# Expert gathers one expert further ahead, and a down product in split one-pass parts

## The chip, the cores and the metric

The kernel runs on one core of a Trainium2 chip. The time is the device time of one launch in microseconds. The number of a kernel is the median of several runs. The profile is one execution, recorded by the hardware profiler.

## What is computed

A network of two blocks for one sequence of 512 tokens of width 1024. The first block has two layers; each mixes the tokens by latent attention, an mLSTM and a state-space scan, and ends in a mixture of 16 experts in four groups. The second block has layers with a gated delta rule, a linear recurrence and a feed-forward part. The change touches the experts of the first block alone:

```python
def _hier_moe(x, wg, bg, we, be, w_gate, w_up, w_down):
    glog = (jnp.einsum('bsd,dg->bsg', x, wg) + bg).astype(F32)
    gp, gi = lax.top_k(jax.nn.softmax(glog, -1), 1)
    ...
    ep, ei = lax.top_k(jax.nn.softmax(elog, -1), TOP_K)
    ep = ep / jnp.sum(ep, -1, keepdims=True)
    eid = gi * EXPERTS_PER_GROUP + ei
    combine = jnp.sum(jax.nn.one_hot(eid, N_EXPERTS, dtype=F32) * (gp * ep)[..., None], axis=2)
    h = jax.nn.silu(jnp.einsum('bsd,edf->bsef', x, w_gate)) * jnp.einsum('bsd,edf->bsef', x, w_up)
    h = h * combine[..., None].astype(h.dtype)
    return jnp.einsum('bsef,efd->bsd', h, w_down)
```

Each token goes to two of the 16 experts. An expert has gate and up weights of 1024 x 256 each and down weights of 256 x 1024, all fp32.

## The kernel before

All engines run the stage `experts` as five queues of their own, written out by hand and joined by semaphores; nothing reorders them. The stage runs once per layer (its outer loop makes one pass when no expert has more than 128 tokens, as here), over experts e = 0 to 15.

For one expert, in the order of the data:

- **GpSimd** gathers up to 128 rows of the tokens into XE by an indirect DMA (`gather`, L1174); XE has two buffers, so gather e waits until expert e-2 has been transposed (`row_t`). The row numbers are in `table`.
- **SyncE** loads the gate/up weights (GU, 2 MB, four buffers, two of them in the tile `raw`, one in XT) and the down weights (DN, 1 MB, four buffers).
- **TensorE** transposes XE into a bank (`rows_t`, L1204). ScalarE copies it as a rounded high part XS (L1278) and VectorE writes the rest as the low part (L1321). The weights are split likewise: ScalarE's `high` (L1271) and VectorE's `low` (L1315) fill WS, each half of an expert in one 128x2048 instruction.
- **TensorE** multiplies in 24 one-pass matmuls (`gate_up_of`, L1216): high x high, high x low and low x high, listed in `TERMS`. ScalarE applies silu (L1295), VectorE multiplies gate and up into H (L1357), TensorE transposes H (`hidden_t`, L1226), ScalarE copies it to HT (L1307).
- **TensorE** forms the down product (`down_of`, L1237) in plain fp32, 4 matmuls which the trace shows as 8. ScalarE copies the lower half to YE and VectorE the upper one (`out_home`, L1284 and L1328).
- **GpSimd** scatters YE to the table `mixed_dram` (`scatter`, L1181).

The index of the rows comes from TensorE (`table_of`, L1245), from one-hot rows that VectorE writes (`hot_rows`, L1334), and VectorE turns it into integers (`index`, L1338).

What sets the order: in round e, TensorE does gate/up of e, the table of e+3, down of e-1, the transposes of rows e+2 and then of H e. GpSimd does gather e+3, then scatter e. ScalarE does the first half of `high` of e+1, silu e, the second half, YE of e-1, the XS of e+2, HT of e.

Of the kernel before, what the change touches and what calls it, by code (L numbers as in the profile page):

```python
# [1136 lines left out]
def experts(nc, m, r, layer):  # L1137
# [7 lines left out]
    names = ("hot_row", "table_done", "indexed", "dve_step", "xe_in0", "xe_in1", "ye_out0", "ye_out1", "gu_in0", "gu_in1", "gu_in2", "gu_in3", "dn_in0", "dn_in1", "dn_in2", "dn_in3", "row_t", "xe_high", "xe_low",  # L1145
             "w_high", "w_low", "gate_up", "silu_done", "hidden", "ht_done", "ht_home", "down", "ye_act", "ye_dve")
    with stage(nc, "experts", *names) as (block, sems):
        hot_row, table_done, indexed, dve_step, xe_in0, xe_in1, ye_out0, ye_out1, gu_in0, gu_in1, gu_in2, gu_in3, dn_in0, dn_in1, dn_in2, dn_in3, row_t, xe_high, xe_low, \
            w_high, w_low, gate_up, silu_done, hidden, ht_done, ht_home, down, ye_act, ye_dve = sems
        xe_in, ye_out = (xe_in0, xe_in1), (ye_out0, ye_out1)  # L1150
        gu_in, dn_in = (gu_in0, gu_in1, gu_in2, gu_in3), (dn_in0, dn_in1, dn_in2, dn_in3)
        GU = KD * S

        @block.sync
        def _(sp):

            for e in range(NE):
                b = e % 4

                if e >= 4:  # L1160
                    sp.wait_ge(w_low, 2 * (e - 3))
                sp.dma_start(r.GU[b], m.d["w_exp"][bass.ds(layer, 1), e, :, 0:GU].rearrange("a p n -> p (a n)")).then_inc(gu_in[b], 16)
                if e >= 4:
                    sp.wait_ge(down, 2 * (e - 3))
                sp.dma_start(r.DN[:, b, :], m.d["w_exp"][bass.ds(layer, 1), e, :, GU:].rearrange("a p n -> p (a n)")).then_inc(dn_in[b], 16)

        @block.gpsimd
        def _(pool):
# [9 lines left out]
            def scatter(e):  # L1178
                pool.wait_ge(ye_act, e + 1)
                pool.wait_ge(ye_dve, e + 1)  # L1180
# [15 lines left out]
        def _(pe):  # L1196
# [24 lines left out]
            def hidden_t(e):  # L1221
                pe.wait_ge(hidden, e + 1)
                if e:
                    pe.wait_ge(ht_home, e)
# [1414 lines left out]
```

## Time and profile before

| | us |
|---|---|
| median of 3 runs | 2199.01 (2198.95 to 2201.67) |
| the profiled execution | 2196.01 |
| its span, first to last instruction | 2194.2 |
| TensorE busy in the span | 1761.4 (80%) |
| VectorE, ScalarE, GpSimd busy | 1099.9, 804.6, 675.9 |
| mean granted TensorE clock | 0.896 |

The busy shares are means over stages with different limits, so they say little about one stage. The two expert stages together take under a fifth of the span; what counts is which wait in them ends last. A line number is that of the kernel before. "Idle before" is an engine's idle time ahead of an instruction, with what ended it.

### The profile page before, as it was taken

The page shows a single profiled execution, that of the slowest core. Times are in us where ns is not written, and L with a number is a line of the kernel's source. Part 1 is how long each engine was busy: PE and PEld are TensorE (multiplying, and loading weights), DVE is VectorE, ACT ScalarE, POOL GpSimd, SP SyncE. Part 2 cuts the span into 40 slices and gives each one's busy share as a digit, 9 for nine tenths or more (in the row PEclk, how much of TensorE's full clock was granted, in tenths as well). Part 3 has the DMA queues.
Part 4 walks back from the last instruction along what each step waited for, and adds up shares of the span by engine and source line. Part 5 has one row for each costly group of instructions (what it writes and reads, how often), then busy time and mean ns, then how long its engine had stood idle before and what let it go on. Part 6 is the DMA issues. An engine that isn't in the chain of part 4 may idle for free. (4 is left out here: it accounts for less than half of the span.)

```text
span 2194.2 us, 22094 instructions
## 1 busy us (share of the span) xinstructions
PE 1761.4 (80%) x7850; PEld 1318.8 (60%) x7850; DVE 1099.9 (50%) x1623; ACT 804.6 (37%) x1196; POOL 675.9 (31%) x351
## 2 busy tenths in 40 slices
PE   4999885759991899986858893499697487999997
PEld 3876533646660786731646661488377376888885
DVE  2836565455656555654646665391455413242241
ACT  2246554134542235665215452322635322111111
POOL 2426524011110444632301110243342113444442
PEclk9999996869995999997959996799789798999998
DMA  4201111077744311020148862320000204222221
GB/s 168 77 31 39 44 34 58 39 292 304 307 165 156 121 48 41 1 77 20 39 178 346 318 255 112 116 96 23 18 1 1 72 6 154 96 96 96 96 76 48
DMA packets 40473, 233.80 MB, mean 107 GB/s; under 512 B 9316, under 2 KB 9700, under 8 KB 20660
## 3 DMA queue, kind: packets, MB, share of 16 engines
q1 hardware_dynamic: 31012, 215.42, 26.1%
q0 software_dynamic: 9216, 16.80, 2.0%
q8 instruction: 59, 0.97, 0.2%
q10 hardware_dynamic: 144, 0.26, 0.1%
q14 instruction: 42, 0.34, 0.1%
HBM read 226.00 MB, written 23.23 MB: 114 GB/s over the span
## 5 line engine op out<-in xcount | busy, mean ns | idle before, releaser
L2134 POOL TENSOR_TENSOR WS<-ring,WS 128x2048 fp32r<-128x2048 f32 x32 | 154.6, 4833 | 228.5 <-ACT WS L2126 228.5
L252 PE MATMUL bank<-XS,WS 128*128 128x512 f32 x864 | 201.8, 396 | 19.9 <-POOL WS L448 19.9
L252 PEld LDWEIGHTS bank<-XS,WS 128*128 128x128 f32 x864 | 165.3, 192 | 56.0 <-POOL WS L448 21.2
L1216 PE MATMUL bank<-WS,XS 128*128 128x512 f32 x768 | 190.3, 405 | 2.2 <-DVE XS L1321 2.2
L2155 PE MATMUL bank<-XS,WS 128*128 128x512 f32 x768 | 177.1, 393 | 14.3 <-POOL WS L2134 14.3
L2173 PE MATMUL bank<-WS,US 128*128 128x512 f32 x768 | 174.7, 389 | 0.0
L2155 PEld LDWEIGHTS bank<-XS,WS 128*128 128x128 f32 x768 | 145.7, 190 | 44.9 <-issue 14.5
L1216 PEld LDWEIGHTS bank<-WS,XS 128*128 128x128 f32 x768 | 147.3, 195 | 33.3 <-DVE XS L1321 3.0
L2126 ACT CAST WS<-ring 128x2048 fp32r<-128x2048 f32 x32 | 61.2, 1913 | 283.2 <-PE bank L2155 150.0
L2173 PEld LDWEIGHTS bank<-WS,US 128*128 128x128 f32 x768 | 144.2, 188 | 29.9
L1519 PE MATMUL bank<-XS,WS 128*128 128x512 f32 (+1 forms) x600 | 138.6, 394 | 13.9 <-POOL WS L1573 13.9
L1519 PEld LDWEIGHTS bank<-XS,WS 128*128 128x128 f32 (+1 forms) x600 | 112.3, 187 | 39.8 <-POOL WS L1573 14.1
L448 POOL TENSOR_TENSOR WS<-raw,WS 128x2048 fp32r<-128x2048 f32 x20 | 92.9, 4646 | 110.9 <-ACT WS L306 110.8
L1181 POOL DMA_INDIRECT mixed_rows<-YE,table x32 | 32.2, 1005 | 288.1 <-DVE YE L1328 147.0
L1237 PE MATMUL bank<-DN,HT 128*128 128x512 f32 x256 | 117.2, 600 | 1.0 <-issue 1.0
L662 POOL TENSOR_SCALAR XT<-XT,RC 128x512 f32<-128x512 f32 x64 | 100.2, 1567 | 46.9 <-DVE RC L627 46.7
L961 PE MATMUL bank<-WS,XS 128*128 128x512 f32 x384 | 92.8, 406 | 26.4 <-POOL WS L1022 26.4
L1315 DVE TENSOR_TENSOR WS<-raw,WS 128x2048 fp32r<-128x2048 f32 x32 | 73.2, 2291 | 60.5 <-ACT WS L1271 60.5
L961 PEld LDWEIGHTS bank<-WS,XS 128*128 128x128 f32 x384 | 75.7, 198 | 45.8 <-issue 29.5
L2204 DVE TENSOR_TENSOR X<-X,bank 128x512 f32<-128x512 f32 x32 | 22.0, 688 | 144.4 <-PE bank L2173 144.4
L1573 POOL TENSOR_TENSOR WS<-ring,WS 128x2048 fp32r<-128x2048 f32 (+1 forms) x13 | 58.8, 4524 | 76.1 <-ACT WS L1530 76.1
L183 PE MATMUL bank<-ident,X 128*128 128x128 f32 x128 | 23.2, 367 | 70.6 <-issue 48.0
(472 smaller groups left out, 3346.3 us busy)
## 6 DMA issues: line engine op xcount, KB each, us to landing
raw<-in_w_exp SPq DMA_DIRECT2D x16, 2048.0 KB, 10.6
DN<-in_w_exp SPq DMA_DIRECT2D x32, 1024.0 KB
ring<-in_w_ff SPq DMA_DIRECT2D x32, 1024.0 KB, 4.8
raw<-in_w_in SPq DMA_DIRECT2D x20, 1024.0 KB, 4.9
GU<-in_w_exp SPq DMA_DIRECT2D x8, 2048.0 KB, 10.5
XT<-in_w_exp SPq DMA_DIRECT2D x8, 2048.0 KB, 10.4
ring<-in_w_in SPq DMA_DIRECT2D x12, 1024.0 KB, 4.8
raw<-in_w_out SPq DMA_DIRECT2D x8, 1024.0 KB, 5.0
```

The costliest lines, as they stand in the source:

```text
L252: last = pe.matmul(m.ps[g % 8][:, :], WS[:, i % 2, hw, at:at + P], XS[:, hx, k, :], start=(step == 0), stop=(step == 3 * KD - 1))
L448: pool.tensor_tensor(WS[:, i % 2, 1, :], m.raw[:, i % 4, :], WS[:, i % 2, 0, :].bitcast(F32), ALU.subtract).then_inc(w_low, 1)
L662: pool.tensor_scalar(PR[:, i % 4, :], PR[:, i % 4, :], a.RC[:, i % 4:i % 4 + 1], None, ALU.mult).then_inc(probs_normed, 1)
L961: last = pe.matmul(m.ps[2 * t + half][:, :], XS[:, hx, 4 * kh + k, t * P:(t + 1) * P], WS[:, 2 * kh + half, hw, k * S:(k + 1) * S], start= ...
L1216: last = pe.matmul(m.ps[2 + e % 2][:, :], r.XS[:, e % 2, hx, 4 * half + k, :], r.WS[:, half, hw, k * S:(k + 1) * S], start=(half == 0 and ...
L1237: last = pe.matmul(m.ps[5 + half][:, :], r.HT[:, e % 2, f * P:(f + 1) * P], r.DN[:, e % 4, at:at + S], start=(f == 0), stop=(f == 1))
L1315: dve.tensor_tensor(r.WS[:, half, 1, :], r.GU[e % 4][:, half * 4 * S:(half + 1) * 4 * S], r.WS[:, half, 0, :].bitcast(F32), ALU.subtract). ...
L1519: last = pe.matmul(m.ps[u % 8][0:n, :], q.WS[:, i % 2, hw, at:at + n], b.XS[:, hx, k, :], start=(step == 0), stop=(step == 3 * KD - 1))
L2126: act.copy(f.WS[:, q % 2, 0, :], f.ring[:, q % 4, :]).then_inc(w_high, 1)
L2134: pool.tensor_tensor(f.WS[:, q % 2, 1, :], f.ring[:, q % 4, :], f.WS[:, q % 2, 0, :].bitcast(F32), ALU.subtract).then_inc(w_low, 1)
L2155: last = pe.matmul(m.ps[mine + u % 4][:, :], f.WS[:, q % 2, hw, k * 256 + c * P:k * 256 + (c + 1) * P], f.XS[:, hx, k, :], start=(n == 0), ...
L2173: last = pe.matmul(bank[:, :], f.US[:, hx, 4 * kh + k, t * P:(t + 1) * P], f.WS[:, q % 2, hw, k * S:(k + 1) * S], start=(kh == 0 and n == ...
```

## The change

Three things change in the stage `experts`.

1. The gathers: GpSimd issues gather e+4 in round e (and gather 3 in round 0), ahead of scatter e. The table, the one-hot rows and the index of e+4 move to round e on TensorE and VectorE with it.
2. The down product: HT and the down weights are split into a high and a low part. HT's high part is ScalarE's copy, its low part a subtraction on VectorE. DN's high part is written by ScalarE (`part_high`, two 128x1024 casts), its low part by GpSimd (`part_low`, two 128x1024 subtractions, between gather e+4 and scatter e). The parts lie in the new tile DS, which has one buffer, and TensorE does 12 one-pass matmuls. HT has one buffer for each part.
3. The rest: both halves of YE are copied by ScalarE. DN has two buffers instead of four; SyncE loads DN e after the low part of e-2 is written, and GU e+2 behind it.

In the rows below, numbers at the start are lines of the kernel they belong to.

GpSimd at the start of the stage, before (XE is the gather, mixed_rows the scatter):

```order
L1167 UNCONDITIONAL_BRANCH
L1174 DMA XE<-x_rows,table 128x1024 x4
L1181 DMA mixed_rows<-YE,table 1024x1024
L1174 DMA XE<-x_rows,table 128x1024
L1181 DMA mixed_rows<-YE,table 1024x1024
```

and after:

```order
L1171 UNCONDITIONAL_BRANCH
L1178 DMA XE<-x_rows,table 128x1024 x5
L1192 TENSOR_TENSOR DS<-DN,DS 128x1024 x2
L1185 DMA mixed_rows<-YE,table 1024x1024
L1178 DMA XE<-x_rows,table 128x1024
L1192 TENSOR_TENSOR DS<-DN,DS 128x1024 x2
```

Five gathers now stand ahead of the first scatter, and two subtractions stand between each gather and the next scatter.

ScalarE over one expert in the middle of the stage, before (WS: gate/up weights, high part; GB: silu; XS: rows, high part):

```order
L1271 CAST WS<-raw 128x2048
L1295 ACTIVATE GB<-bank 128x256
L1271 CAST WS<-raw 128x2048
L1284 COPY YE<-bank 128x512
L1278 CAST XS<-bank 128x512 x2
L1307 COPY HT<-bank 128x256
```

and after:

```order
L1290 CAST WS<-raw 128x2048
L1322 ACTIVATE GB<-bank 128x256
L1290 CAST WS<-raw 128x2048
L1304 COPY YE<-bank 128x512 x2
L1297 CAST XS<-bank 128x512 x2
L1334 CAST HT<-bank 128x256
L1311 CAST DS<-DN 128x1024 x2
```

The two casts of the down weights stand behind HT, ahead of the next expert's weights.

The diff, cut to its core:

```diff
@@ sync
-            for e in range(NE):
-                b = e % 4
-
+            def gate_up_in(e):
                 if e >= 4:
                     sp.wait_ge(w_low, 2 * (e - 3))
...
+            gate_up_in(0)
+            gate_up_in(1)
+            for e in range(NE):
+                if e >= 2:
+                    sp.wait_ge(down_low, 2 * (e - 1))
+                sp.dma_start(r.DN[:, e % 2, :], m.d["w_exp"][bass.ds(layer, 1), e, :, GU:].rearrange("a p n -> p (a n)")).then_inc(dn_in[e % 2], 16)
+                if e + 2 < NE:
+                    gate_up_in(e + 2)
@@ gpsimd
+            def part_low(e):
+                for f in range(2):
+                    pool.wait_ge(down_high, 2 * e + f + 1)
+                    cols = slice(f * D, (f + 1) * D)
+                    pool.tensor_tensor(r.DS[:, 1, cols], r.DN[:, e % 2, cols], r.DS[:, 0, cols].bitcast(F32), ALU.subtract).then_inc(down_low, 1)
...
             for e in range(NE):
-                if e + 3 < NE:
-                    gather(e + 3)
+                if e == 0:
+                    gather(3)
+                if e + 4 < NE:
+                    gather(e + 4)
+                part_low(e)
                 scatter(e)
@@ tensor
             def down_of(e):
-                pe.wait_ge(dn_in[e % 4], 16 * (e // 4 + 1))
-                pe.wait_ge(ht_home, e + 1)
+                pe.wait_ge(ht_low, e + 1)
                 for half in range(2):
                     if e:
-                        pe.wait_ge((ye_act, ye_dve)[half], e)
+                        pe.wait_ge((ye_low, ye_up)[half], e)
+                    n = 0
                     for f in range(2):
+                        if half == 0:
+                            pe.wait_ge(down_low, 2 * e + f + 1)
                         at = f * D + half * S
-                        last = pe.matmul(m.ps[5 + half][:, :], r.HT[:, e % 2, f * P:(f + 1) * P], r.DN[:, e % 4, at:at + S], start=(f == 0), stop=(f == 1))
+                        for hw, hx in TERMS:
+                            last = pe.matmul(m.ps[5 + half][:, :], r.HT[:, hx, f * P:(f + 1) * P], r.DS[:, hw, at:at + S], start=(n == 0), stop=(n == 5))
+                            n += 1
                     last.then_inc(down, 1)
@@ scalar
             def out_home(e):
...
+                for half in range(2):
+                    act.wait_ge(down, 2 * e + half + 1)
+                    if e >= 2:
+                        act.wait_ge(ye_out[e % 2], 16 * (e // 2))
+                    act.copy(r.YE[:, e % 2, half * S:(half + 1) * S], m.ps[5 + half][:, :]).then_inc((ye_low, ye_up)[half], 1)
+
+            def part_high(e):
+                act.wait_ge(dn_in[e % 2], 16 * (e // 2 + 1))
+                if e:
+                    act.wait_ge(down, 2 * e)
+                for f in range(2):
+                    act.copy(r.DS[:, 0, f * D:(f + 1) * D], r.DN[:, e % 2, f * D:(f + 1) * D]).then_inc(down_high, 1)
...
                 act.wait_ge(ht_done, e + 1)
-                if e >= 2:
-                    act.wait_ge(down, 2 * (e - 1))
-                act.copy(r.HT[:, e % 2, :], m.ps[4][:, 0:2 * P]).then_inc(ht_home, 1)
+                if e:
+                    act.wait_ge(down, 2 * e)
+                act.copy(r.HT[:, 0, :], m.ps[4][:, 0:2 * P]).then_inc(ht_high, 1)
+                part_high(e)
@@ vector
-            def out_home(e):
-                dve.wait_ge(down, 2 * e + 2)
...
+                dve.wait_ge(ht_high, e + 1)
+                if e:
+                    dve.wait_ge(down, 2 * e)
+                dve.tensor_tensor(r.HT[:, 1, :], m.ps[4][:, 0:2 * P], r.HT[:, 0, :].bitcast(F32), ALU.subtract).then_inc(ht_low, 1)
```

## Rows read from the trace of the kernel before

**Rows 1.** Waits in the expert stages, layer one, then two: total, times, longest.

```profile
PE bank L1204 <- DMA XE<-x_rows,table: 15.3, 11, 3.6
...
PE bank L1204 <- DMA XE<-x_rows,table: 17.2, 12, 3.2
```

**Rows 2.** Timeline of one period: start, length, engine, line, operation, idle before.

```profile
566.94 5.72 PE L1216 MATMUL bank<-WS,XS 128*128 128x512 f32 x24
...
568.24 1.01 POOL L1174 DMA_INDIRECT XE<-x_rows,table  x1 [0.31 <-issue]
...
570.03 1.91 ACT L1271 CAST WS<-raw 128x2048 fp32r<-128x2048 f32 x1 [2.11 <-PE bank L1216]
...
572.86 3.68 PE L1237 MATMUL bank<-DN,HT 128*128 128x512 f32 x8
...
574.90 2.29 DVE L1315 TENSOR_TENSOR WS<-raw,WS 128x2048 fp32r<-128x2048 f32 x1 [0.30 <-ACT WS L1271]
...
577.18 0.68 DVE L1328 COPY YE<-bank 128x512 f32<-128x512 f32 x1
...
577.37 1.09 PE L1204 MATMUL bank<-ident,XE 128*128 128x128 f32 x8 [0.83 <-DMA XE<-x_rows,table]
...
578.06 1.07 ACT L1278 CAST XS<-bank 128x512 fp32r<-128x512 f32 x2 [2.62 <-PE bank L1204]
...
578.43 5.72 PE L1216 MATMUL bank<-WS,XS 128*128 128x512 f32 x24
...
578.72 1.01 POOL L1181 DMA_INDIRECT mixed_rows<-YE,table  x1 [9.46 <-PE bank L1204]
579.02 0.39 ACT L1307 COPY HT<-bank 128x256 f32<-128x256 f32 x1
...
580.03 1.02 POOL L1174 DMA_INDIRECT XE<-x_rows,table  x1 [0.31 <-issue]
```

**Rows 3.** Timeline of TensorE near the end of layer one's stage.

```profile
630.49 3.59 PE L1237 MATMUL bank<-DN,HT 128*128 128x512 f32 x8
633.92 1.04 PE L1204 MATMUL bank<-ident,XE 128*128 128x128 f32 x8
```

**Rows 4.** Timeline: first gate/up matmul, gather of expert 3, last scatter, layer one.

```profile
467.89 0.80 PE L1216 MATMUL bank<-WS,XS 128*128 128x512 f32 x1 [1.01 <-DVE XS L1321]
...
483.05 0.99 POOL L1174 DMA_INDIRECT XE<-x_rows,table  x1 [14.34 <-DVE table L1338]
...
659.17 0.97 POOL L1181 DMA_INDIRECT mixed_rows<-YE,table  x1 [3.42 <-DVE YE L1328]
```

**Rows 5.** Durations elsewhere: first ns min/median/max, then busy us, mean ns.

```profile
L448 POOL TENSOR_TENSOR WS<-raw,WS x20: 4499/4618/4847, 35.4 to 813.9; 128x2048 fp32r<-128x2048 f32 x20
...
L653 POOL TENSOR_TENSOR QS<-QT,QS 128x512 fp32r<-128x512 f32 x14 | 17.9, 1282 | 0.0
...
L1450 ACT ACTIVATE XN<-X 128x1024 f32<-128x1024 f32 x8 | 8.3, 1043 | 27.6 <-PEq L76 21.7 <-PEq L2403 5.9
```

**Rows 6.** Output projection: GpSimd and VectorE side by side; VectorE's min/median/max.

```profile
361.37 4.52 POOL L1022 TENSOR_TENSOR WS<-raw,WS 128x2048 fp32r<-128x2048 f32 x1 [14.38 <-ACT WS L1007]
...
361.84 4.60 DVE L973 TENSOR_TENSOR XS<-XT,XS 128x512 fp32r<-128x512 f32 x1 [1.39 <-ACT XS L1002]
...
L973 DVE TENSOR_TENSOR XS<-XT,XS x16: 683/2646/5104, 358.0 to 1055.7; 128x512 fp32r<-128x512 f32 x16
```

**Rows 7.** TensorE after two pauses; in between a window: length, busy, PEclk, DMA, GB/s.

```profile
518.09 1.67 PE L1204 MATMUL bank<-ident,XE 128*128 128x128 f32 x8 [1.98 <-DMA XE<-x_rows,table]
...
519.84 6.66 PE L1216 MATMUL bank<-WS,XS 128*128 128x512 f32 x24
...
520.00:522.00 2.00, 2.00 (x6) 1.58 (x6) 1.72 (x6) 0.66 (x2) 0.62 (x1) 0.54 1.08 459
...
1185.97 1.09 PE L1204 MATMUL bank<-ident,XE 128*128 128x128 f32 x8 [3.23 <-DMA XE<-x_rows,table]
```

**Rows 8.** Window at the start of layer one's stage; last columns PEclk, DMA share, GB/s.

```profile
470.00:500.00 30.00, 25.07 (x106) 19.17 (x106) 15.88 (x23) 14.56 (x17) 3.03 (x3) 0.88 0.98 403
```

More of the change, by code:

```diff
@@ L1137, in experts @@
 def experts(nc, m, r, layer):
[L1145 to L1146 removed]
+    names = ("hot_row", "table_done", "indexed", "dve_step", "xe_in0", "xe_in1", "ye_out0", "ye_out1", "gu_in0", "gu_in1", "gu_in2", "gu_in3", "dn_in0", "dn_in1", "row_t", "xe_high", "xe_low",
+             "w_high", "w_low", "gate_up", "silu_done", "hidden", "ht_done", "ht_high", "ht_low", "down_high", "down_low", "down", "ye_low", "ye_up")
     with stage(nc, "experts", *names) as (block, sems):
[L1148 to L1149 removed]
+        hot_row, table_done, indexed, dve_step, xe_in0, xe_in1, ye_out0, ye_out1, gu_in0, gu_in1, gu_in2, gu_in3, dn_in0, dn_in1, row_t, xe_high, xe_low, \
+            w_high, w_low, gate_up, silu_done, hidden, ht_done, ht_high, ht_low, down_high, down_low, down, ye_low, ye_up = sems
         xe_in, ye_out = (xe_in0, xe_in1), (ye_out0, ye_out1)
[L1151 removed]
+        gu_in, dn_in = (gu_in0, gu_in1, gu_in2, gu_in3), (dn_in0, dn_in1)
         GU = KD * S
@@ L1155, in _ @@
         def _(sp):
-            for e in range(NE):
-                b = e % 4
+            def gate_up_in(e):
                 if e >= 4:
                     sp.wait_ge(w_low, 2 * (e - 3))
[L1162 to L1165, printed above, removed]
+                sp.dma_start(r.GU[e % 4], m.d["w_exp"][bass.ds(layer, 1), e, :, 0:GU].rearrange("a p n -> p (a n)")).then_inc(gu_in[e % 4], 16)
+            gate_up_in(0)
[6 more added lines that the diff above has]
+                    gate_up_in(e + 2)
         @block.gpsimd
@@ L1223, in hidden_t @@
                 if e:
-                    pe.wait_ge(ht_home, e)
+                    pe.wait_ge(ht_low, e)
                 for f in range(2):
@@ L1254, in _ @@
                     rows_t(1)
-                if e + 3 < NE:
-                    table_of(e + 3)
+                if e == 0:
+                    table_of(3)
+                if e + 4 < NE:
+                    table_of(e + 4)
                 if e:
@@ L1280, in out_home @@
             def out_home(e):
-                act.wait_ge(down, 2 * e + 1)
-                if e >= 2:
-                    act.wait_ge(ye_out[e % 2], 16 * (e // 2))
-                act.copy(r.YE[:, e % 2, 0:S], m.ps[5][:, :]).then_inc(ye_act, 1)
+                for half in range(2):
[9 more added lines that the diff above has]
+                    act.copy(r.DS[:, 0, f * D:(f + 1) * D], r.DN[:, e % 2, f * D:(f + 1) * D]).then_inc(down_high, 1)
             high(0, 0)
@@ L1349, in _ @@
             for e in range(NE):
-                if e + 3 < NE:
-                    hot_rows(e + 3)
+                if e == 0:
+                    hot_rows(3)
+                if e + 4 < NE:
+                    hot_rows(e + 4)
                 if e + 1 < NE:
@@ L1361, in _ @@
                     low(e + 1, 1)
-                if e + 3 < NE:
-                    index(e + 3)
-                if e:
-                    out_home(e - 1)
+                if e == 0:
+                    index(3)
+                if e + 4 < NE:
+                    index(e + 4)
                 if e + 2 < NE:
                     rows_low(e + 2)
-            out_home(NE - 1)
+                dve.wait_ge(ht_high, e + 1)
+                if e:
+                    dve.wait_ge(down, 2 * e)
+                dve.tensor_tensor(r.HT[:, 1, :], m.ps[4][:, 0:2 * P], r.HT[:, 0, :].bitcast(F32), ALU.subtract).then_inc(ht_low, 1)
             dve.wait_ge(hot_row, NE * NT)
```

13 lines of the change are left out of this document (5 added, 8 removed).

## The prediction

> **What bounds the kernel now.** I read the views in this order: the waits of the expert stages, the timeline of one expert in steady state, then durations, first and last instructions, and the granted clock. The only thing TensorE waits for repeatedly there is the gathered rows XE: 15.3 us in layer one, 17.2 in layer two [rows 1]. The timeline shows why [rows 2]. One expert runs from the gate/up matmuls at 566.94 to those at 578.43, 11.49 us: 5.92 to the first down matmul, then the down product, then a wait of 0.83 until XE lands, then 1.06 from the transposes (577.37) to the next gate/up. Those transposes use a gather issued at 568.24, 9.1 us earlier. That gather stands behind the scatter of an earlier expert, which waits for VectorE's copy of YE (577.18 in this period), which waits its turn behind VectorE's low part of the weights (574.90). So two loops are nearly equal: TensorE's own work and the gather behind the scatter. Where XE was in time, the down product is 3.43 long from start to start [rows 3], so TensorE alone would take 5.92 + 3.43 + 1.06 = 10.4. GpSimd does 2.3 us of work per expert and is otherwise idle. The stage of layer one runs from 467.89 to the start of its last scatter, 659.17: 191.3 us [rows 4]; layer two is taken alike.
>
> **What the change removes.** Gather e+4 is queued ahead of scatter e. Its own condition (the transposes of e+2 are done) is met about one period earlier than now, so XE has a period of slack beside its 9.1 us and the waits of [rows 1] go. The down product becomes 12 one-pass matmuls. At 5.72/24 = 0.238 each [rows 2] they take 2.86 in place of 3.43, a gain of 0.57. VectorE loses a 0.68 copy. If nothing else came, TensorE's period would be 5.92 + 2.86 + 1.06 = 9.84.
>
> **What it adds.** ScalarE gets a second YE copy (half of the 1.07 for two XS parts [rows 2], 0.55) and two 128x1024 casts; the only 128x1024 row without bias is 1.04 [rows 5], taken as 1.0. VectorE gets a 128x256 subtraction from a bank, hidden while it waits. GpSimd gets two 128x1024 subtractions. Their price lies between half of the fastest 128x2048 one, 2.25, and the line through 1.28 for 512 and 4.62 for 2048, 2.39, a little more if disturbed [rows 5]; I take 2.35. On SyncE, DN(e) waits for the subtractions of e-2, and the gate/up weights of e+2 are queued behind it, so they are requested about 20 us ahead of use where now it is over three periods. Both transfers with a gather and a scatter are some 3.7 MB, 9.2 us at the 403 GB/s of [rows 8]. I count nothing for them: about 8 us are left, and a period longer than now relieves the queue.
>
> **The new loop.** GpSimd works in order: scatter, gather, low part f0, low part f1. Time 0 is the end of f1 of one expert.
> - TensorE, released by f1, has 9 of 12 down matmuls left: 0.15 + 9 x 0.238 = 2.3. (0.15 is my estimate for one release: the XS copy starts 0.69 after the transposes, of which half take 0.54 [rows 2].)
> - ScalarE copies the second half of YE: 0.15 + 0.55, at 3.0. The scatter starts 0.86 after YE (577.86 to 578.72 [rows 2]): 3.86. The gather starts 1.31 later and takes 1.02: 6.2. Then f0 starts at 6.35. The gap of 0.15 is an estimate between 0.05 and the 0.31 between two transfers.
> - f0 ends at 8.7. Without interference f1 ends at 11.05.
>
> ScalarE's casts don't limit f0. The HT copy is over 2.04 after the transposes start [rows 2], at 4.34, the casts at 5.35 and 6.35.
>
> **Interference.** VectorE's low part of WS (L1315) reads two SBUF operands and takes 2.29 [rows 2]. In the output projection VectorE runs such an instruction, XS<-XT,XS, beside GpSimd's WS<-raw,WS. Alone it takes 0.68. Started 0.47 after GpSimd's it takes 4.60, and ends 0.55 after GpSimd's end, with a maximum of 5.10 [rows 6]. So they exclude one another, instruction by instruction, and take turns. The Trainium skill, "SBUF — State Buffer", section "SBUF: two separate sides", says that such a pair is an exclusive lock held for the whole instruction and names VectorE operations with two SBUF inputs. By its wording VectorE's reads of a bank stay free, which no row I use shows; if they too had to wait, the sum would be some 1 us per expert higher.
>
> Where does the request fall? The transposes start at 2.3, gate/up at 3.36. ScalarE's first cast of the next weights starts 3.09 after that (566.94 to 570.03 [rows 2]), at 6.45, and ends at 8.36. VectorE asks at 8.4, while f0 holds the lock until 8.7. VectorE goes next, until 11.0; f1 then runs to **13.35**. The second VectorE part is ready at about 11.4 and waits for f1, harmlessly, since gate/up of the next expert starts 3.36 after f1. Period 13.35 against 11.49 now, and TensorE pauses about 3.5 us inside each down product (three matmuls done at 10.0, resumed at 13.5).
>
> **Sum of a stage**, from the first gate/up matmul:
> - First f1: gather 3 starts at 15.2 [rows 4], gather 4 is over at 17.5, and f0 and f1 need 4.7 with one or two VectorE parts between: 24.6 to 26.5 or a little less; 25.
> - 11 periods of 13.35: 146.9.
> - Two periods without a gather: f0 follows the first cast at 5.5 and f1 ends at 10.2, before VectorE gets its turn; 10.3 each, 20.6. Two more, also without transposes: 9.75 each, 19.5.
> - From the last f1 to the last scatter: 0.15 + 2.14 + 0.15 + 0.55 + 0.86 = 3.85.
>
> Together 215.8, against 191.3: +24.5 per layer, **+49**. The profiled execution took 2196.0 (span 2194.2), the median is 3.0 higher: 2199.0 + 49 = **2248**.
>
> **Rivals.**
> - **VectorE just misses f0** (ask after 8.7; the margin is 0.3). Then f1 ends at 11.05, but VectorE's parts and the index behind them slip, the next gather starts 0.9 late, and in the next period VectorE is in time: 14.2. Mean 12.6. That saves 0.75 x 11 x 2 = 16: 2232; with the lower prices of both bounds (2.25 and 0.05) about 2216. For it: the small margin. Against: slips on GpSimd help VectorE be in time.
> - **No price for the lock** (the other side). If the two engines don't collide here, the period is 11.05, the first f1 at 22.3: 22.3 + 121.6 + 20.6 + 19.5 + 3.85 = 187.9, so 3.4 less per layer: 2192. GpSimd's loop has then replaced the gather's, almost at the same length, and the longer tail (f0 and f1 behind the last scatters) eats most of the gain. It decides if VectorE's request falls after f1 has begun in every period. Against it: [rows 6].
> - **TensorE becomes the bound**, if GpSimd's subtractions overlapped its transfers or weren't waited for: 9.84, so 1.65 less over 13 periods and some 3 us per layer for the longer waits of the first experts (up to 3.6 [rows 1]): 2199 - 49 = 2150. Against it: one queue in order.
> - **The clock falls in the pauses.** After a pause of 1.98 the granted clock was 0.54, the 1.2 GHz level: the transposes took 1.67 in place of 1.09, the 24 matmuls 6.66 in place of 5.72, together 1.5. After one of 3.23 it didn't fall and they took 1.09 [rows 7]. The new pause is 3.5, in 13 periods per layer. Half of them: +20, 2268; all of them: +39, 2287. A dearer subtraction (2.5) or a gap of 0.31 adds 3 to 4 us per layer.
> - **The gather isn't further ahead in effect:** XE has two buffers as before. It still starts a period earlier, and even at 15 us to landing it would be in time, so this costs nothing.
>
> **Chances.** The lock with VectorE in time 0.50 (2248, by the prices' bounds 2235 to 2262); just missing 0.17 (2216 to 2232); falls of the clock or dearer GpSimd work on top 0.21 (2262 to 2290); no price for the lock 0.09 (2192); TensorE the bound 0.03 (2150). The range leaves out the last two and the end of the clock's case: 2212 to 2284. A measurement of this kernel tells about 0.2%, 4.4 us, from no change. Faster: 0.03 and over half of 0.09, 0.08; same: the rest of it, and a little of the second case, 0.05; slower 0.87.
>
> **What would show it.** In the profile after: the wait for XE gone; TensorE waiting for GpSimd's DS inside the down product in nearly every expert; GpSimd's second 128x1024 subtraction recorded at about 4.6 and the first at 2.35; VectorE's low part of WS sometimes 2.29, sometimes longer; periods of about 13.35, then four shorter; granted clock at 1.00 for most of the stage. I would be wrong if the subtractions were both at 2.3 (no lock), if periods alternated between 11 and 14, or if TensorE waited for something else: weights that land late, or ScalarE.

## The result and the profile after

| | before | after |
|---|---|---|
| median, same chip | 2199.52 us (2198.95 to 2201.67) | 2255.85 us (2250.22 to 2257.06) |
| the profiled execution / its span | 2196.01 / 2194.2 | 2250.22 / 2248.5 |
| mean granted clock | 0.896 | 0.876 |
| experts, layer one, first gate/up to last scatter | 191.3 | 216.8 |
| experts, layer two | 190.1 | 216.7 |

The ratio is 1.0249, interval 1.0230 to 1.0268: slower, by 56 us. Of the 54.3 us that the span grew, 25.5 and 26.6 are the two stages. The other 2.2 lie outside them: 0.8 more ahead of the first stage, 2.0 more ahead of the second, 0.6 less behind it. In layer one gather 0 lands 10.7 us after its issue instead of 9.2; a second load of gate/up weights now stands ahead of DN 0.

Three groups of the page of the changed kernel, GpSimd's subtraction, the down product and VectorE's one-hot rows (busy us, mean ns | idle before and who ended it):

```profile
L1192 POOL TENSOR_TENSOR DS<-DN,DS 128x1024 fp32r<-128x1024 f32 x64 | 151.2, 2387 | 1.0
...
L1253 PE MATMUL bank<-DS,HT 128*128 128x512 f32 x384 | 133.0, 507 | 18.6 <-POOL DS L1192 18.6
...
L1356 DVE TENSOR_SCALAR HOT<-IOTA,POS 128x128 fp32r<-128x128 f32 x128 | 138.5, 1150 | 3.1 <-PEq L76 3.1
```

The subtraction costs what was expected. The third row wasn't expected: a one-hot row, a 128x128 tile, takes 1150 ns in the mean, where most take 280. TensorE's waits over the whole run of the changed kernel (total, times, longest) point at the same rows:

```profile
PE bank L1262 <- DVE HOT L1356: 50.1, 22, 5.6
...
PE bank L1217 <- DMA XE<-x_rows,table: 18.8, 2, 9.5
PE bank L1253 <- POOL DS L1192: 18.6, 12, 4.8
PE bank L1262 <- DVE table L1360: 11.3, 6, 5.0
```

The wait for XE of [rows 1] has gone: two are left, each stage's very first. In its place TensorE waits 22 times for a one-hot row. It waits for DS only 12 times, though the prediction had it wait in nearly every expert.

One period of the changed kernel, from its timeline (start, length, engine, line, operation, idle before); it answers to [rows 2]:

```profile
566.12 6.01 DVE L1356 TENSOR_SCALAR HOT<-IOTA,POS 128x128 fp32r<-128x128 f32 x4
566.25 1.05 POOL L1178 DMA_INDIRECT XE<-x_rows,table  x1 [0.31 <-issue]
567.32 4.73 POOL L1192 TENSOR_TENSOR DS<-DN,DS 128x1024 fp32r<-128x1024 f32 x2
...
569.83 0.39 PE L1262 MATMUL bank<-VAL,HOT 128*128 128x2 f32 x3
...
572.06 2.28 DVE L1343 TENSOR_TENSOR WS<-raw,WS 128x2048 fp32r<-128x2048 f32 x1
572.19 0.27 PE L1262 MATMUL bank<-VAL,HOT 128*128 128x2 f32 x1 [1.97 <-DVE HOT L1356]
...
572.33 4.58 PE L1253 MATMUL bank<-DS,HT 128*128 128x512 f32 x12
...
576.94 0.59 ACT L1304 COPY YE<-bank 128x512 f32<-128x512 f32 x1 [1.45 <-PE bank L1253]
...
578.39 1.01 POOL L1185 DMA_INDIRECT mixed_rows<-YE,table  x1 [6.35 <-PE bank L1217]
...
579.71 1.05 POOL L1178 DMA_INDIRECT XE<-x_rows,table  x1 [0.31 <-issue]
580.79 4.72 POOL L1192 TENSOR_TENSOR DS<-DN,DS 128x1024 fp32r<-128x1024 f32 x2
...
585.51 2.28 DVE L1343 TENSOR_TENSOR WS<-raw,WS 128x2048 fp32r<-128x2048 f32 x1
```

Narrow windows of the same timeline split two of these rows, the last one-hot row and the first subtraction:

```profile
580.17 5.42 DVE L1356 TENSOR_SCALAR HOT<-IOTA,POS 128x128 fp32r<-128x128 f32 x1
```

```profile
580.79 2.40 POOL L1192 TENSOR_TENSOR DS<-DN,DS 128x1024 fp32r<-128x1024 f32 x1
```

The two subtractions are called f0 and f1 as in the prediction, the DMA of GpSimd ahead of them is the gather. Read from the end of f1 at 572.05 (567.32 + 4.73): 0.28 until the down product starts, 4.61 until ScalarE's copy of YE (576.94), 0.59 for the copy, 0.86 to the scatter, 1.32 to the gather, 1.08 to f0, 4.72 for f0 and f1. Together **13.46**, and seven of the stage's intervals between gate/up starts are of this length. The two subtractions run back to back, undisturbed. What is held up is VectorE: it asked for its fourth one-hot row 0.46 us after the gather began, and the row ended only when gather, f0 and f1 were over. TensorE's table product (L1262) needs that row, and it stands in TensorE's queue ahead of the down product, so none of the 12 matmuls runs before f1's end. The first three rows had got through.

The clock, in windows (length, busy PE, PEld, DVE, ACT, POOL with counts, granted clock, DMA share, GB/s):

```profile
572.00:573.00 1.00, 0.81 (x4) 0.66 (x5) 1.00 (x2) 0.20 (x1) 0.04 (x1) 0.87 0.00 0
573.00:574.00 1.00, 1.00 (x4) 0.81 (x3) 1.00 (x1) 0.00 (x0) 0.00 (x0) 0.50 0.89 164
...
576.00:577.00 1.00, 1.00 (x7) 0.82 (x6) 0.94 (x2) 0.06 (x1) 0.00 (x0) 0.92 1.10 467
```

After the pause of 1.97 the granted clock falls to 0.50, the 1.2 GHz level, for about the length of the down product: 12 matmuls take 4.58. At 519.70, in a shorter round of the same stage and at a granted clock of 1.00, they take 3.00. In the nine longest rounds of layer one (13.4 or more) they take 4.5 to 5.5, together 15 us more than at 3.00 each, out of the 25.5 that the stage grew. The clock is back at full before gate/up.

At the stage's start, two rows in the first round, one of VectorE and one of TensorE, from the timeline:

```profile
480.53 2.29 DVE L1343 TENSOR_TENSOR WS<-raw,WS 128x2048 fp32r<-128x2048 f32 x1 [0.64 <-ACT WS L1290]
...
482.94 1.01 PE L1262 MATMUL bank<-VAL,HOT 128*128 128x2 f32 x4 [4.95 <-DVE table L1360]
```

Round 0 now makes two tables. The second must wait until VectorE has read the first, and that `index` stands in VectorE's queue behind a low part of the weights. TensorE stands for 4.95 us.

### The profile page after: what moved, and what is told of

Its sections match the earlier page's. It is cut to its first block and busy times, and to the rows that moved or that the text cites. A ratio compares the mean times of both kernels' runs of the same rounds, so it can differ in the third digit from the quotient of the medians.

```text
span 2248.5 us, 22572 instructions
## 1 busy us (share of the span) xinstructions
PE 1777.6 (79%) x7978; PEld 1369.4 (61%) x7978; DVE 1210.7 (54%) x1623; ACT 882.6 (39%) x1292; POOL 831.5 (37%) x415
## 5 line engine op out<-in xcount | busy, mean ns | idle before, releaser
L1192 POOL TENSOR_TENSOR DS<-DN,DS 128x1024 fp32r<-128x1024 f32 x64 | 151.2, 2387 | 1.0
L1253 PE MATMUL bank<-DS,HT 128*128 128x512 f32 x384 | 133.0, 507 | 18.6 <-POOL DS L1192 18.6
L1356 DVE TENSOR_SCALAR HOT<-IOTA,POS 128x128 fp32r<-128x128 f32 x128 | 138.5, 1150 | 3.1 <-PEq L76 3.1
L1253 PEld LDWEIGHTS bank<-DS,HT 128*128 128x128 f32 x384 | 93.1, 251 | 45.5 <-POOL DS L1192 13.9
```

The lines of the kernel that those rows point to most:

```text
L1192: pool.tensor_tensor(r.DS[:, 1, cols], r.DN[:, e % 2, cols], r.DS[:, 0, cols].bitcast(F32), ALU.subtract).then_inc(down_low, 1)
L1253: last = pe.matmul(m.ps[5 + half][:, :], r.HT[:, hx, f * P:(f + 1) * P], r.DS[:, hw, at:at + S], start=(n == 0), stop=(n == 5))
L1356: dve.tensor_scalar(r.HOT[:, e % 2, t, :], m.IOTA[:, :], r.POS[:, t, e:e + 1], None, ALU.is_equal).then_inc(hot_row, 1)
```

## The experiments

Two theories stood at the outset. **Turns**, the prediction's: VectorE and GpSimd exclude one another and take turns, so VectorE's low part of the weights gets in between f0 and f1. **No turn**, formed from the profile: VectorE gets no turn between GpSimd's back-to-back instructions; the one-hot row is blocked from the gather to f1's end, and because the table stands ahead of the down product, the whole product and a fall of the clock go onto GpSimd's loop.

| kernel | median us | ratio to before (95%) | stages, layer one / two |
|---|---|---|---|
| gathers alone | 2180.40 | 0.9887 to 0.9931 | 177.0 / 177.1 |
| split alone | 2259.36 | 1.0263 to 1.0297 | 217.0 / 215.4 |
| one-hot rows moved | 2222.05 | 1.0087 to 1.0121 | 202.5 / 201.1 |
| table behind down product | 2229.38 | 1.0111 to 1.0172 | 205.2 / 206.1 |
| subtractions in quarters | 2338.74 | 1.0587 to 1.0655 | 246.5 / 248.4 |
| gather between f0 and f1, rows moved | 2243.35 | 1.0160 to 1.0233 | 212.5 / 211.0 |
| fills instead of subtractions | 2223.67 | 1.0070 to 1.0140 | 201.3 / 201.2 |
| the same, rows moved | 2225.35 | 1.0066 to 1.0147 | 197.2 / 202.3 |
| low parts on VectorE | 2170.46 | 0.9862 to 0.9896 | 170.2 / 170.1 |
| low parts on VectorE, index earlier | 2162.89 | 0.9799 to 0.9841 | 167.5 / 167.4 |
| gathers alone, index earlier | 2165.26 | 0.9814 to 0.9860 | 173.5 / 173.6 |
| low parts on VectorE, index earlier, loads reordered | 2160.20 | 0.9788 to 0.9832 | 168.3 / 168.1 |

The ratios are to the kernel before as it was measured again beside each kernel (medians 2198.85 to 2201.88); the stages are those of the profiled executions. A stage's length is the sharper measure: the granted clock in the code ahead of it, which the change leaves as it is, differs between the profiles, and the first stage starts anywhere from 467 to 476 (474 to 476 where the clock from 300 to 350 us was 0.76, 467 to 471 where it was 0.79 to 0.84), the second 488 to 497 after the end of the first. Rounds are counted from one start of gate/up to the next.

### The two parts, each alone

The kernel before with the gathers, tables, one-hot rows and indices of the change:

```diff
@@ gpsimd (tensor and vector alike)
-                if e + 3 < NE:
-                    gather(e + 3)
+                if e == 0:
+                    gather(3)
+                if e + 4 < NE:
+                    gather(e + 4)
                 scatter(e)
```

> The kernel before with the gathers (and the table, one-hot rows and index with them) one expert further ahead, nothing else. If the waits for XE are what the profile of before shows, they vanish and TensorE's own 10.4 us per expert remain: about 15 us less per layer, although the first round gets 5 us longer, since the table of expert 4 now waits for the index of expert 3 (4.95 us in the changed kernel). That gives about 2170. Rival: the transfers (3.7 MB per expert at 403 GB/s, 9.2 us) or the weights come late at that pace, and the gain shrinks to under 10 us in all, 2190 or more.

Measured 2180.40, 0.9% faster. Between the first and the last rounds its intervals are 10.4, ten times in a row, the length that the prediction gave TensorE alone. Of the waits of [rows 1] one is left in layer one:

```profile
PE bank L1206 <- DMA XE<-x_rows,table: 7.3, 1, 7.3
```

It is the stage's very first. The first round takes 17.2 here too, as the second table waits for the first index; the expectation had counted that. The two stages are 27.3 shorter, near the 30 expected. But the profiled execution is only 15.5 shorter: the first stage starts 5.9 later than before, and 7.5 more lie between the two, in code that is the same. Whether that comes with the change or is the spread between executions isn't known.

The changed kernel with the gathers back at e+3, on all three engines:

```diff
-                if e == 0:
-                    gather(3)
-                if e + 4 < NE:
-                    gather(e + 4)
+                if e + 3 < NE:
+                    gather(e + 3)
                 part_low(e)
```

> The changed kernel with the gathers back at three experts ahead: the split down product alone. If GpSimd's loop (scatter, gather, two subtractions, VectorE's one-hot rows behind them, the down product) sets the period, 13.4 us stay, XE lands in time at that pace anyway, and only the first round gets shorter by the 4.95 us that TensorE waited for the index of expert 3: about 2246. Rival: the shorter distance brings waits for XE back, 1 us or more per expert, 2270 or more.

Measured 2259.36, period 13.45, stages of 217.0 and 215.4. The whole loss is the split's. The gathers, worth 13 to 14 us a stage alone, bring nothing beside it: GpSimd's loop contains its gather wherever the gather's number stands. The first round is shorter (12.5), as expected, but one more long round makes up for it, so the 2246 expected didn't come.

### Who is blocked, and who waits behind it

The one-hot rows moved out of GpSimd's busy stretch, to just behind `index`:

```diff
                 if e == 0:
                     hot_rows(3)
-                if e + 4 < NE:
-                    hot_rows(e + 4)
+                    hot_rows(4)
...
                     index(e + 4)
+                if e + 5 < NE:
+                    hot_rows(e + 5)
```

> The changed kernel with VectorE's one-hot rows written one round earlier, in the idle 1.1 us ahead of its XS low parts, when GpSimd computes nothing. Theory of the shared port as predicted: TensorE no longer waits for the one-hot rows, but VectorE's low part of the weights, now asked for during GpSimd's first subtraction, gets its turn between the two, so the second subtraction is recorded at about 4.6 us and the period stays near 13.35 (or 12.6 where it alternates): 2235 to 2255. Rival: only the one-hot rows are blocked, and the low parts of the weights run beside GpSimd at 2.28; then the period is GpSimd's own 11.1 to 11.3 and the time about 2203.

Measured 2222.05, between what the theory (2235 to 2255) and its rival (2203) gave: 34 us of the loss are gone, but the rounds alternate between 13.2 and 10.8, mean 12.0. The timeline of one round:

```profile
570.97 4.72 POOL L1192 TENSOR_TENSOR DS<-DN,DS 128x1024 fp32r<-128x1024 f32 x2
...
572.33 5.51 DVE L1343 TENSOR_TENSOR WS<-raw,WS 128x2048 fp32r<-128x2048 f32 x1 [1.22 <-ACT WS L1290]
...
573.50 0.94 PE L1253 MATMUL bank<-DS,HT 128*128 128x512 f32 x3 [0.15 <-POOL DS L1192]
...
575.74 2.54 PE L1253 MATMUL bank<-DS,HT 128*128 128x512 f32 x6 [1.30 <-POOL DS L1192]
```

This is the prediction's own situation: VectorE asks for a low part of WS at 572.33, while f0 runs. It got no turn between f0 and f1. It lasted 5.51, until 2.15 behind f1's end, and f0 and f1 together took their 4.72. That refutes "turns" for this pair. "No turn" has the blocking right but didn't foresee the rest: the nine matmuls behind f1 (the view ends at 578) took 3.82 at a lower clock (0.56 in the window 576 to 578), and in the 10.8 rounds 2.34 after a shorter pause. Such falls make up 1.5 of the 2.4 between the two kinds of round. The one-hot rows' blocking is real: moving them alone was worth 1.5%.

The rows stay, and TensorE's table moves behind the down product:

```diff
-                if e + 4 < NE:
-                    table_of(e + 4)
                 if e:
                     down_of(e - 1)
+                if e + 4 < NE:
+                    table_of(e + 4)
```

> The changed kernel, GpSimd's subtractions and VectorE's order as they are, with TensorE's table matmuls of expert e+4 queued behind the down product of e-1 instead of ahead of it. The one-hot rows stay blocked (5.4 us), but no down product stands behind them. If that queue order is how the port costs time, the down product starts at once, its pause falls from 2.0 before all 12 matmuls to one before the last nine, the clock falls less often, and the period goes from 13.46 to 11.2 to 12.0: 2195 to 2222. Rival: VectorE's weights, held back by the same blocking, come late for the next gate/up; then it stays above 2240.

Measured 2229.38, 26 us less than the changed kernel and a little outside what was expected. VectorE's rows are blocked as long as ever, but three matmuls now run before f1's end, so that nine are left:

```profile
572.14 5.83 DVE L1356 TENSOR_SCALAR HOT<-IOTA,POS 128x128 fp32r<-128x128 f32 x4
...
577.73 2.34 PE L1253 MATMUL bank<-DS,HT 128*128 128x512 f32 x9 [0.98 <-POOL DS L1192]
```

In other rounds of this kernel the nine matmuls take 3.91, at the lower clock, and its intervals spread from 10.4 to 14.0. So what stands behind the blocked row in TensorE's queue carries about half of the loss, with GpSimd's 4.7 us as they were.

### What kind of exclusion

Each subtraction cut into four, to offer VectorE more boundaries:

```diff
-                    pool.tensor_tensor(r.DS[:, 1, cols], r.DN[:, e % 2, cols], r.DS[:, 0, cols].bitcast(F32), ALU.subtract).then_inc(down_low, 1)
+                    for c in range(4):
+                        cols = slice(f * D + c * 256, f * D + (c + 1) * 256)
+                        last = pool.tensor_tensor(r.DS[:, 1, cols], r.DN[:, e % 2, cols], r.DS[:, 0, cols].bitcast(F32), ALU.subtract)
+                    last.then_inc(down_low, 1)
```

> The changed kernel with each of GpSimd's two 128x1024 subtractions cut into four of 128x256 (0.6 us each), back to back. In the changed kernel and with the one-hot rows moved, VectorE waited through both subtractions though there was a boundary between them. Theory A: GpSimd keeps the pair as long as its instructions follow back to back; then nothing changes but the fixed cost of six more instructions, VectorE's fourth one-hot row still takes about 5.4 us, and the time is 2256 or slightly more. Theory B: VectorE gets its turn at any boundary and missed the only one by accident of timing; with seven boundaries its longest one-hot row falls under 2 us, TensorE no longer waits for the table, and the time falls to 2235 or less.

The letters there aren't this section's order: its theory A is "no turn", its B is "turns".

Measured 2338.74, 6% slower than before; rounds alternate between 11.9 and 18.75. Its timeline, one round of each kind:

```profile
567.71 6.40 DVE L1358 TENSOR_SCALAR HOT<-IOTA,POS 128x128 fp32r<-128x128 f32 x4
...
568.25 5.57 POOL L1193 TENSOR_TENSOR DS<-DN,DS 128x256 fp32r<-128x256 f32 x8
...
581.11 9.71 POOL L1193 TENSOR_TENSOR DS<-DN,DS 128x256 fp32r<-128x256 f32 x8
...
583.15 2.31 DVE L1345 TENSOR_TENSOR WS<-raw,WS 128x2048 fp32r<-128x2048 f32 x1 [0.45 <-ACT WS L1292]
```

In the first kind a one-hot row, asked for at 568.10 while the gather runs, waits through all eight pieces (5.82). In the second, one-hot rows are served between pieces (0.77 each), VectorE's low part of WS too, and GpSimd's eight take 9.71 instead of 5.57. Neither theory holds as stated: a boundary between two GpSimd instructions passes the turn in some cases and not in others. What decides it wasn't found.

With the one-hot rows moved as above, the gather placed between f0 and f1:

```diff
+                part_low(e, 0)
                 if e + 4 < NE:
                     gather(e + 4)
-                part_low(e)
+                part_low(e, 1)
                 scatter(e)
```

> The kernel with the one-hot rows moved (2222), and the gather of e+4 placed between GpSimd's two subtractions instead of ahead of them. If the pair is free while GpSimd writes the descriptors of a gather (1 us), VectorE's low part of the weights starts in that gap and then holds the second subtraction off for its 2.28 us: the second subtraction is recorded at 3 us or more, VectorE's at 2.3 to 3.5 in place of 4.7 to 5.5. By the sum of the loop (f1 later by about 2.3) the time would be 2235 to 2250. Rival: the gather holds VectorE off as well, nothing is lost to a turn, and the time stays near 2222.

Measured 2243.35, in the range expected; rounds of 14.2 and 11.2. Two rounds of its timeline differ by half a microsecond in when VectorE asks:

```profile
566.35 1.02 POOL L1178 DMA_INDIRECT XE<-x_rows,table  x1
...
566.93 4.99 DVE L1343 TENSOR_TENSOR WS<-raw,WS 128x2048 fp32r<-128x2048 f32 x1 [3.39 <-ACT WS L1290]
...
577.96 1.02 POOL L1178 DMA_INDIRECT XE<-x_rows,table  x1 [0.16 <-issue]
578.06 2.29 DVE L1343 TENSOR_TENSOR WS<-raw,WS 128x2048 fp32r<-128x2048 f32 x1 [1.22 <-ACT WS L1290]
579.01 3.54 POOL L1191 TENSOR_TENSOR DS<-DN,DS 128x1024 fp32r<-128x1024 f32 x1
```

Asked 0.10 after the gather's start, VectorE is served at once and f1 is held up (3.54 instead of 2.37). Asked 0.58 after it, VectorE waits through the rest of the gather and all of f1. So a turn can be had shortly after a gather's start, and not later. By itself a gather costs little: in the kernel before, with no subtraction behind it, no one-hot row took more than 0.50, asked 0.54 after the gather's start and done at its end.

```profile
L1334 DVE TENSOR_SCALAR HOT<-IOTA,POS x128: 266/279/503, 453.0 to 1293.4; 128x128 fp32r<-128x128 f32 x128
```

GpSimd's subtractions replaced, from expert 1 on, by three fills of a spare tile (about 0.97, 0.97 and 0.43 us), which read nothing and leave the low part of the down weights out:

```diff
+                    else:
+                        scratch(slice(0, D))
+                        scratch(slice(0, D))
+                        scratch(slice(0, 400))
+                        pool.wait_ge(pool_step, scratched[0])
+                        pool.sem_inc(down_low, 1)
```

> The changed kernel, but from expert 1 on GpSimd fills a spare 128x1024 tile (some 2.3 us of fills in place of each subtraction) and reads nothing; the low part of the down weights is left at that of expert 0, so that part of the computation is left out. GpSimd is as long busy, so its loop stays. If it is reading SBUF that blocks VectorE, the one-hot rows are free, TensorE doesn't wait for the table, the clock stays up, and the period is GpSimd's own 11.1 to 11.3: 2200 to 2210. If writing blocks the one-hot rows as well (they run at two elements a cycle), it stays at 2245 to 2260.

And the same with the one-hot rows moved:

> The same fills in place of the subtractions (the same part of the computation left out), with the one-hot rows moved out of GpSimd's way. What may still collide is VectorE's low part of the weights, with two SBUF inputs. If such an instruction is held off only by a GpSimd instruction that reads SBUF, it takes 2.28 us every time and the time is 2195 to 2208, GpSimd's loop alone; if also by one that writes, it takes 4.5 to 5.5 as with the subtractions and the time is near 2222.

Measured 2223.67 and 2225.35. The first lies between its two ranges; the second is where its rival had it (near 2222), but not for the rival's reason. The groups of the first (ns least, median, most; first and last start) and one row of its timeline show what the fills block:

```profile
L1371 DVE TENSOR_SCALAR HOT<-IOTA,POS x128: 276/282/2445, 452.3 to 1299.4; 128x128 fp32r<-128x128 f32 x128
...
L1358 DVE TENSOR_TENSOR WS<-raw,WS x32: 2283/2293/2293, 462.0 to 1316.4; 128x2048 fp32r<-128x2048 f32 x32
```

```profile
568.89 1.83 DVE L1371 TENSOR_SCALAR HOT<-IOTA,POS 128x128 fp32r<-128x128 f32 x1
```

Instructions that only write still block a one-hot row (one tensor operand in SBUF): the one shown waits for the rest of the gather and one fill, 1.84 at most over the run, and is done 0.09 after that fill. (The 2445 ns are beside expert 0's subtraction, which stays.) Between two fills GpSimd waits for a semaphore and is idle for 0.06, between two subtractions it isn't. Fills never block the low part of WS (two operands in SBUF), though it ran beside them in almost every round: 2293 at most in 32. Against subtractions the same instruction took up to 5.56. So for the two-operand form it is GpSimd's reading that excludes. With rows moved and fills, the period is 11.38, GpSimd's own loop, and layer one's stage 197.2, 5.7 above a loop without exclusion (187.9 by the prediction, plus 11 x 0.33 for the longer period). Part of the rest is the clock: in one round of 13.0 nine matmuls take 3.91 at 0.56, in the others 2.34, after the same pause of 1.35. Layer two has four such rounds and a stage of 202.3, so the median is no better than with the rows in place.

### The low parts elsewhere, and the first round

VectorE writes the low parts of the down weights, behind HT's low part:

```diff
@@ gpsimd
-                part_low(e)
                 scatter(e)
@@ vector
                 dve.tensor_tensor(r.HT[:, 1, :], m.ps[4][:, 0:2 * P], r.HT[:, 0, :].bitcast(F32), ALU.subtract).then_inc(ht_low, 1)
+                part_low(e)
```

> The changed kernel with the low parts of the down weights written by VectorE (2 x 1.15 us) in place of GpSimd, ahead of its one-hot rows. GpSimd computes nothing, so nothing can block VectorE. If GpSimd's subtractions are the cause, directly or through the port, the loss goes and the gain of the shorter down product shows: periods of 10.0 to 10.5, 2160 to 2175. Rival: the loss is in the split itself (ScalarE's added 2.6 us, the single buffer DS, the later requests of the weights): then it stays above 2220.

Measured 2170.46, 1.2% faster than before, as expected. The rest of the split is as in the changed kernel, so ScalarE's added work, the single buffer DS and the later loads aren't what cost the time. One period (9.76: gate/up at 561.10 and 570.86) of its timeline:

```profile
563.10 2.36 DVE L1349 TENSOR_TENSOR DS<-DN,DS 128x1024 fp32r<-128x1024 f32 x2
...
565.38 0.87 DVE L1355 TENSOR_SCALAR HOT<-IOTA,POS 128x128 fp32r<-128x128 f32 x4
...
567.03 2.98 PE L1246 MATMUL bank<-DS,HT 128*128 128x512 f32 x12
```

VectorE does both subtractions in 2.36, half of GpSimd's 4.72, the four one-hot rows take 0.87, and the 12 matmuls 2.98 at full clock. TensorE is the bound again, at 9.76 where the prediction's rival had 9.84.

The index of expert 3 ahead of VectorE's second low part of the first round, in that kernel and in the one with the gathers alone:

```diff
-                if e + 1 < NE:
-                    low(e + 1, 1)
                 if e == 0:
                     index(3)
+                if e + 1 < NE:
+                    low(e + 1, 1)
```

> The kernel with the low parts on VectorE (2170), and in round 0 the index of expert 3 taken ahead of VectorE's second low part of the weights instead of behind it. TensorE's table of expert 4 waits for that index, 4.9 us in the first round. If that wait is real time, 2 to 3 us less per layer: 2164 to 2167. Rival: the gather of expert 2 lands at about the same moment and the first rounds stay as long: 2170.

> The kernel with the gathers alone further ahead (2180), with the same earlier index of expert 3: 2174 to 2178, or 2180 if the first rounds are bound by the gather.

Measured 2162.89 and 2165.26, the first a little under its range, the second clearly. The first interval is 13.8 in both instead of 16.6 and 17.2, and the stages are 2.8 and 3.5 shorter. Of the 15 us that the second median fell, the stages account for 7; its first stage starts 6.7 earlier than with the gathers alone. Between these two kernels the split with VectorE's low parts is worth 6.0 and 6.2 us a stage; the medians differ by 2.4 with overlapping intervals, so in the whole time it isn't shown.

Last, the kernel with the low parts on VectorE and the index earlier, with SyncE's first three loads in the order of the kernel before: GU 0, DN 0, GU 1, then GU 2, DN 1, GU 3.

```diff
             gate_up_in(0)
-            gate_up_in(1)
             for e in range(NE):
+                if e == 1:
+                    gate_up_in(2)
...
-                if e + 2 < NE:
+                if e == 0:
+                    gate_up_in(1)
+                elif e + 2 < NE and e >= 2:
                     gate_up_in(e + 2)
+                elif e == 1:
+                    gate_up_in(3)
```

> The low parts on VectorE, the early index, and the down weights of expert 0 loaded ahead of the gate/up weights of expert 1, as in the kernel before, so that the first gather meets less traffic (it took 1.2 to 1.5 us longer to land in the changed kernel). 1 us less per layer than with the early index alone: 2162 to 2165, under both kernels and about 1.6% under the kernel before. Rival: the gate/up weights of expert 1 are then late for ScalarE and the time is that of the early index alone or above.

Measured 2160.20, ratio 0.9810 (0.9788 to 0.9832), the lowest median of all and 1.9% under the kernel before. Against the one without the reordering the intervals overlap, so its gain isn't shown: from the issue of gather 0 to gate/up it takes 11.8 and 12.6 instead of 13.3 and 13.7, but the stages are 0.9 and 0.8 longer.

## Why the prediction was nearly right, and where it wasn't

It said 2248 (2212 to 2284); it was 2255.85. Of the 8 us between, 3 are the stages (+25.5 and +26.6 where it had +24.5 for each), 2 what lies outside them, and 3 that the profiled execution of the changed kernel lies 5.6 under its median, not 3.0.

That the period came out within 0.11 is luck, as two wrong terms cancel; the rest of the sum isn't.

**Right.** The waits for XE went. GpSimd in order, scatter, gather, f0, f1, is the new loop. The prices held: subtractions 2.39 (2.35), casts 1.0 each, 0.86 from YE to the scatter, 1.32 from there to the gather (1.31), YE's copy 0.59 (0.55). The first f1 ended 23.8 after the first gate/up matmul (25), the stage took 216.8 (215.8), the period 13.46 (13.35). The two engines exclude one another, as [rows 6] showed. (Its lower bounds, 2235 and 2216, don't follow from its prices: 0.1 less for each subtraction and for the gap is some 8 us in all, which gives 2240 and 2224. Nothing hangs on it.)

**Wrong: the composition of the period.** Two terms failed, with opposite signs and nearly the same size.

- *"So they exclude one another, instruction by instruction, and take turns"*, with VectorE from 8.7 to 11.0 between f0 and f1: 2.3 us that didn't exist. In the period shown, VectorE's low part of WS began only at f1's end. Where it did ask during f0 (one-hot rows moved), it had to wait until after f1. The changed kernel has the predicted case itself, in the first round without one-hot rows: VectorE asks 2.16 after f0's start, where the prediction had 2.05, f0 and f1 take their 4.74, and VectorE ends 2.16 behind them.

```profile
634.48 4.74 POOL L1192 TENSOR_TENSOR DS<-DN,DS 128x1024 fp32r<-128x1024 f32 x2
...
636.64 4.73 DVE L1343 TENSOR_TENSOR WS<-raw,WS 128x2048 fp32r<-128x2048 f32 x1 [3.17 <-ACT WS L1290]
```

- *"TensorE, released by f1, has 9 of 12 down matmuls left: 0.15 + 9 x 0.238 = 2.3."* It had all 12, at 1.2 GHz, behind the last bit of the table: from f1's end to YE's copy 0.28 + 4.61 = 4.89, where the prediction has 0.15 + 2.14 + 0.15 = 2.44. Of the 2.45 more, 1.58 is the clock (4.58 against 3.00) and 0.71 the three matmuls.

So +2.45 stood in for −2.3. The prediction said that f1 would be recorded at about 4.6; it is at 2.35. Its own sign of being wrong, *"if the subtractions were both at 2.3 (no lock)"*, came true, though the exclusion is there: it shows on VectorE's instructions instead.

**What was overlooked.** The change moves one-hot rows and table of e+4 with the gathers, and the prediction costed only the gather. It weighed VectorE's instruction with two SBUF operands and no other. The one-hot row, 0.28 us by itself, is asked for 0.4 to 0.6 after the gather's start in every long round and lasts 5.3 to 5.4; the table behind it holds the down product. The Trainium skill, "SBUF — State Buffer", section "SBUF: two separate sides", gives the port pair that the two engines share to whichever starts first, for a whole instruction, and names VectorE's 2-port modes beside the two-input form; the rows agree that both forms are held up by subtractions (5.42 and 5.51), and by fills only the one-hot row (1.84, against 2.29 for the low part of WS, its length alone). That a held instruction waits through several of GpSimd's, 5.42 over a gather and two subtractions, is more than one whole instruction.

**The rival of the clock** had 0.21 and a pause of 3.5 in mind. The pause became 1.97, close to the 1.98 of [rows 7], and the clock fell in every long round, as it had there. As its effect ended with the down product, it cost 1.6 a round there, about as much as the 1.5 on transposes and gate/up that the rival had. So the rival's mechanism was at work in a time that the forecast reached without it.

**A second miss, nearly without effect:** the table of expert 4 waits 4.95 for the index of expert 3 in round 0 (first interval 17.2, before 12.2), but the wait for XE in the next round goes (10.7, before 14.3). The experiment that moved `index` shows 3 us a stage in it.

**Still open** is the rule by which a boundary between two GpSimd instructions passes the turn. It didn't for a one-hot row asked for during the gather (through up to eight pieces), nor for the low part of WS between f0 and f1. It did for the same low part between 128x256 pieces, for VectorE's XS in the output projection of [rows 6], and for a one-hot row in the changed kernel's own first round, asked for 0.06 after f0's start and done 0.12 after f1's:

```profile
487.77 2.43 DVE L1356 TENSOR_SCALAR HOT<-IOTA,POS 128x128 fp32r<-128x128 f32 x1
```

For back-to-back subtractions of 128x1024 and 128x2048 the 14 traces sort by when VectorE asks. In all 90 cases within 0.54 of a subtraction's start (as in [rows 6], 0.47) it had the turn at that subtraction's end; in all 28 cases from 1.32 on it waited through the next one too. The prediction took [rows 6] over to a request 2.05 after the start. No run moved the request alone, and the 128x256 pieces don't sort that way (0.58 after a piece's start it went either way), so this is a pattern and not a shown cause.

## What to carry to other kernels

Before elementwise work goes to GpSimd, list every instruction that VectorE issues in the same stretch, the tiny ones too, and what stands behind each of them in TensorE's queue; a 0.28 us row that was blocked for 5.4 us held back 12 matmuls, and the pause took the clock down with it. If VectorE has room, the low part belongs there: the same kernel went from 2.5% slower to 1.2% faster by this alone. And when a look-ahead is made longer, follow its helper steps (index, table) through the first round, where two of them meet.

## What the runs showed of the hardware

- A gather on GpSimd (1.0 us of its time) can hold up VectorE's SBUF operations, but not from its start: a low part of WS asked for 0.10 us after it was served at once, one at 0.58 waited. A one-hot row at 0.46 waited 5.4 with subtractions behind the gather, and took 0.28 in the kernel before, with none.
- The other way round too: in all traces a gather or scatter that starts beside VectorE's two-operand subtraction, 0.2 us or more before its end, ends 0.84 to 0.90 after that end, however long it has to wait (1.12 to 2.95 instead of 1.01). One of the kernel with the table moved:

```profile
580.43 2.28 DVE L1343 TENSOR_TENSOR WS<-raw,WS 128x2048 fp32r<-128x2048 f32 x1
...
581.56 2.02 POOL L1185 DMA_INDIRECT mixed_rows<-YE,table  x1 [3.88 <-PE bank L1217]
```

- Cutting GpSimd's work is dear: eight pieces of 128x256 take 5.57 where two of 128x1024 take 4.72.
